# Feed-forward parts of 4, 8, 6 and 4 hidden tiles in a four-layer decoder trunk

## The chip, the cores and the metric

The kernel runs on one core of a Trainium2 chip. The metric is the device time of one execution in microseconds (us); lower is better. Engines: PE is TensorE (matmuls), DVE is VectorE, ACT is ScalarE, POOL is GpSimd, SP is SyncE, which here only issues transfers.

## The reference, cut to what matters

```python
for i in range(4):                       # D = 1024, 512 tokens, one sequence
    h = rmsnorm(x, mix_norm[i])
    x = x + mixer_i(h)                   # i = 0, 3: sparse attention; 1: gated MLP; 2: causal pooling
    x = x + swiglu(rmsnorm(x, ffn_norm[i]), w_gate_up[i], w_down[i])
return rmsnorm(x, final_norm)

def swiglu(h, w_gate_up, w_down):        # 2816 hidden = 22 tiles of 128
    g, u = jnp.split(h @ w_gate_up, 2, axis=-1)
    return (silu(g) * u) @ w_down
```

All of it is float32.

## The kernel before

**Numbers.** A float32 operand is cut into a high part (an ACT copy, rounded) and a low part (a DVE subtraction), and every product is three matmuls: high by high, high by low, low by high (`mm3`, line 2058). Activations stand transposed: a tile is 128 features by 512 tokens. Weights come from memory as 128 rows of up to 1024 columns: DMA into `raw`, ACT writes `w_hi` (line 731), DVE writes `w_lo` (line 1215). There are four such weight slots and four PSUM banks for their results (`RING`), and two slots of `raw`.

**The feed-forward of a layer** goes over its 22 hidden tiles in four parts, `PARTS`. Part 0 (4 tiles) is plain: 8 up blocks of 8 tiles each, then 8 down blocks of 4 tiles each, every matmul 512 columns wide (`first_tiles`, `first_down`). The ups of parts 1, 2 and 3, and the downs of parts 1 and 2, are done with seven products in place of eight (a Strassen-Winograd scheme over 2 by 2 blocks): 256 tokens per matmul, products named s1, s2, a11, s4, s3, a12, a22 (`pair`, line 2172). One up pair is 7 x 4 x 3 = 84 matmuls and makes one hidden tile; one down pair makes two output tiles and is 7 x (half the part's tiles) x 3 matmuls, 63 with a part of 6. The first down pair of a part runs its products in the order s1, a11, s2, s4, s3, a12, a22 (`FIRST_DOWN`), because s2 needs sums of the hidden tile finished last. Those sums and their splits are made by DVE and ACT: `joined` (lines 1461, 1466), `token_sums` (1475 to 1482), `operand_high` (864 to 872), `token_low` (1490), `low` (1503). The weights of a pair are summed and split in four chunks: `pair_sums` (1307, 1309), `pair_high` (787), `pair_low` (1315); GpSimd issues DMAs that add in memory (683, 685).

**The down of part 3** is plain again, eight blocks of (part 3's tiles) x 3 matmuls of 512 columns, with `project`. In this stretch DVE goes, for output tile k, through: the residual (line 1619, one operand in PSUM), the weight split of block k + 3 (line 1215), and the low part of the next norm's input (`xs_low`, line 1223). For k = 3 and k = 7 the last two change places:

```python
if last or k % RING < RING - 1:
    ahead_of(k)
if not last:
    dve.wait_ge(taken, b + 1)
    xs_low(n + 1, k, k + MT * (n + 1))
    if k % RING == RING - 1:
        ahead_of(k)
```

ACT makes the high parts between (lines 731 and 740). GpSimd squares each tile as soon as its residual is in and adds it up (`squares`, lines 627 and 629; 636 for the first). PE opens block b only when its weights are split and when the bank's output of block b - 4 has been taken (`open_block`, line 2067). The mixer that follows reads `xs_lo` tile by tile; the sum of squares is used in its second block. In the last layer there is no `xs_low`; DVE squares tile 7 itself, behind a wait for all of GpSimd's squares (lines 2035 and 2036).

**SBUF.** `xs_hi` and `xs_lo` (8 tiles each) hold the token sums of the hidden tiles in their first 6 tiles and, in tile 7, the high part of one block of tokens, `b21_hi`. `vbd_all` holds attention's compressed values; it is zeroed once, at the start.

Of the kernel before, what the change touches and what calls it, by code (L numbers as in the profile page):

```python
# [25 lines left out]
F32R = mybir.dt.float32r  # L26
# [6 lines left out]
P = 128  # L33
S = 512
D = 1024
MT = D // P
TT = S // P
HEADS, GROUPS, DH = 16, 4, 64
NCMP = 32
HIDDEN_TILES = 22  # L40
PARTS = (4, 6, 6, 6)
TILES_AT = (0, 4, 10, 16)
LAST_PART = len(PARTS) - 1
FIRST_TILES = PARTS[0]
SEQ = [(kind, p, j) for p in range(1, LAST_PART + 1) for kind, n in (("up", PARTS[p]), ("down", MT // 2 * (p < LAST_PART)))
# [5 lines left out]
H = 256  # L51
# [218 lines left out]
def build(nc, x_in, positions, stream, pairs, params, consts, b_s, out, mixers=MIXERS):  # L270
    plan = Plan(mixers)
    ctx = ExitStack()
    with ctx:
# [7 lines left out]
        def over(name, shape, base, at, dt=F32):  # L281

            return nc.alloc_sbuf_tensor_at(name, shape, dt, offset=home[base] + 4 * at)

        def sem(name):
# [53 lines left out]
        t32 = over("t32", [P, 4, 4, H], "mix_lo", 0)  # L339
        part_sums, lin = over("part_sums", [P, 4, H], "tmp", 0), over("lin", [P, 3, H], "tmp", 4 * H)  # L340
        acts = [over("act_e", [P, S], "vstat", 0), over("act_o", [P, S], "hid_lo", (MT - 1) * S)]
        ht32 = over("ht32", [P, 3, 4, H], "xs_lo", 0)

        bank = [ctx.enter_context(nc.psum_tensor(f"bank{i}", [P, S], F32)) for i in range(4)]
        pair = ctx.enter_context(nc.psum_tensor("bank45", [P, 2, S], F32))
# [29 lines left out]

        t_hi = mix_hi[:, :, :].rearrange("p (i k) (h t) -> p i (k h) t", i=4, h=2)
        t_lo = mix_lo[:, :, :].rearrange("p (i k) (h t) -> p i (k h) t", i=4, h=2)
        b21_hi = [xs_hi[:, MT - 1, :].rearrange("p (k t) -> p k t", k=2),
                  xs_lo[:, MT - 1, :].rearrange("p (k t) -> p k t", k=2)]

        ht_hi, ht_lo = (t[:, 0:6, :].rearrange("p (i k) (h t) -> p i (k h) t", i=3, h=2) for t in (xs_hi, xs_lo))

        def hid_11(t, i):

            return t[:, 3 + i // 2, bass.ts(i % 2, H)]

        def f32(ap):
            return ap.bitcast(F32)
# [233 lines left out]
        def _(gp):  # L622
# [72 lines left out]
                    gp.wait_ge(cs_added, e + 1)  # L695
                    nc.gpsimd.tensor_tensor(osum, osum, branch[:, 2, :], ALU.add).then_inc(osum_ready, 1)

            gp.memset(vbd_all[:, :, :, :].rearrange("p g j v -> p (g j v)"), 0.0).then_inc(vbd_zero, 1)
            gp.wait_ge(vbd_zero, 1)
            for j in range(4):  # L700
                gp.memset(vbd_all[NCMP * j:NCMP * (j + 1), :, j, DH:VW], 1.0).then_inc(vbd_zero, 1)
            gp.wait_ge(vbd_zero, 5)
            a = 0
            for l, (kind, _) in enumerate(plan.mixers):
                if norm_of_mixer(l) in cols_of:
                    columns(norm_of_mixer(l))
                if kind == "nsa":
                    nsa(l, a)
                    attention(l, a)
                    a += 1  # L710
                squares(norm_of_ffn(l))
                weight_sums(l)
                squares(norm_of_ffn(l) + 1)
# [1340 lines left out]
        def _(pe):  # L2054
# [3 lines left out]
            def mm3(out_, w, v, start, stop, onto=False):  # L2058

                mm(out_, w[0], v[0], start, False, onto)  # L2060
                mm(out_, w[0], v[1], False, False, onto)
                return mm(out_, w[1], v[0], False, stop, onto)
# [4 lines left out]
            def open_block(b):  # L2067

                pe.wait_ge(w_lo_ready, b + 1)
                if not (type(b) is int and b < RING):  # L2070
                    pe.wait_ge(taken, b - RING + 1)
# [148 lines left out]
            def ffn(l):  # L2220
                n, up = norm_of_ffn(l), plan.ffn[l]

                def amid(k):
                    if k == 2:
                        norm(n)

                project(up, up % RING, MT, xs, (xs_lo_ready, MT * n))
                for b in range(up + 1, up + 2 * FIRST_TILES):
                    project(b, b % RING, MT, xs, before=amid if b == up + 1 else None)
                first_down(l)  # L2230
                for r in range(LAYER_PAIRS):
                    pair(l, r)
                down, t0 = plan.down_block(l, LAST_PART), HIDDEN_TILES * l + TILES_AT[LAST_PART]
                for b in range(down, down + MT):
                    project(b, b % RING, PARTS[LAST_PART], hid, (hid_lo_ready, t0) if b == down else None)

            def values(b0, banks, amid={}, ready=None, spare=0, done=None):

# [507 lines left out]
```

## Time and profile before

| | |
|---|---|
| median of 3 runs | 2320.01 us (2317.48 to 2321.12) |
| the profiled execution | 2318.43 us, its span 2316.3 us |
| PE busy | 2299.5 us (99%), 15224 matmuls |
| DVE, ACT, POOL busy | 1846.0 (80%), 1249.0 (54%), 485.0 us (21%) |
| granted TensorE clock | 9 tenths or more in every slice (mean share 1.0) |
| DMA | 293.12 MB, mean 127 GB/s |

The busy time of PE sums matmuls whose modelled ends overlap, so 99% does not say that PE is at its peak. What one matmul costs in a stream is the distance between two starts in the timeline, and a wait is a distance that is longer than that. The seven-product stretches start at 414.9, 898.2, 1342.2 and 2026.6 us of the span.

### The profile page before, as it was taken

How to read it: one execution, taken by the hardware profiler on the slowest of the kernel's cores; microseconds unless marked ns; L12 is line 12 of the kernel's file. 1: busy time of each engine (PE TensorE's matmuls, PEld its weight loads, DVE VectorE, ACT ScalarE, POOL GpSimd, SP SyncE). 2: the span in 40 equal slices, each digit the busy share in tenths (PEclk: the TensorE clock that was granted, in tenths of full speed). 3: DMA queues.
4: the chain of work that ended last, by engine and by line, in shares of the span. 5: the costliest groups of instructions: out<-in, count | busy, mean ns of one | idle time of the engine just before them, and what ended most of it. 6: DMA issues, size and time to landing. Idle time of an engine off the chain costs nothing.

```text
span 2316.3 us, 41517 instructions
## 1 busy us (share of the span) xinstructions
PE 2299.5 (99%) x15224; PEld 2106.4 (91%) x15224; DVE 1846.0 (80%) x3231; ACT 1249.0 (54%) x2208; POOL 485.0 (21%) x513
## 2 busy tenths in 40 slices
PE   9999999999999999999999999999999999999998
PEld 7889988999988889999988899999889998899997
DVE  8667668899975678999787889997756776989984
ACT  6268744566543344665533455654426783466653
POOL 2211141121130130111133111113320114012112
PEclk9999999999999999999999999999999999999999
DMA  4810014676733245677433467673470002367672
GB/s 162 228 57 2 1 58 120 169 177 167 199 105 109 91 123 140 165 185 192 119 98 101 123 165 177 167 192 110 127 207 29 2 2 94 108 169 185 167 181 91
DMA packets 114242, 293.12 MB, mean 127 GB/s; under 512 B 13184, under 2 KB 25600, under 8 KB 114048
## 3 DMA queue, kind: packets, MB, share of 16 engines
q1 hardware_dynamic: 77904, 229.57, 30.7%
q0 software_dynamic: 35136, 58.74, 15.4%
q8 instruction: 123, 2.02, 0.4%
q10 hardware_dynamic: 1008, 2.21, 0.3%
q14 instruction: 71, 0.58, 0.1%
HBM read 279.98 MB, written 2.10 MB: 122 GB/s over the span
## 4 chain that ended last, share of the span: by engine, by line
PE 92%; DVE 4%; DMA 2%; issue 1%; ACT 1%; SPq 0%; DVEq 0%; ACTq 0%
PE bank L2056 88%; PE bank L2407 3%; DMA raw_b<-pairs 1%; DVE w_lo L1315 1%; DVE act_o L1466 0%; DMA x<-x_in 0%; DVE lin L1588 0%; ACT w_hi L787 0%; DVE lin L1461 0%; DVE xs_lo L1490 0%; PE bank L2437 0%; DVE ht L1479 0%; DVE ht L1477 0%; DVE lin L1593 0%; DVE branch L1821 0%
## 5 line engine op out<-in xcount | busy, mean ns | idle before, releaser
L2056 PE MATMUL bank<-mix_hi,w_hi 128*128 128x256 f32 (+1 forms) x1408 | 428.0, 304 | 0.3
L2056 PE MATMUL bank<-mix_hi,w_lo 128*128 128x256 f32 (+1 forms) x1408 | 425.7, 302 | 0.0
L2056 PE MATMUL bank<-mix_lo,w_hi 128*128 128x256 f32 (+1 forms) x1408 | 425.7, 302 | 0.0
L2056 PE MATMUL bank<-xs_hi,w_hi 128*128 128x512 f32 (+2 forms) x1184 | 412.1, 348 | 6.1 <-DVE xs_lo L1490 5.2
L2056 PE MATMUL bank<-xs_lo,w_hi 128*128 128x512 f32 (+2 forms) x1184 | 404.5, 342 | 0.0
L2056 PE MATMUL bank<-xs_hi,w_lo 128*128 128x512 f32 (+1 forms) x1168 | 398.5, 341 | 0.0
L731 ACT ACTIVATE w_hi<-raw 128x1024 fp32r<-128x1024 f32 (+2 forms) x196 | 186.0, 950 | 229.8 <-DMA raw<-stream 186.1
L1215 DVE TENSOR_TENSOR w_lo<-raw,w_hi 128x1024 fp32r<-128x1024 f32 (+2 forms) x193 | 229.5, 1191 | 95.9 <-ACT w_hi L731 95.3
L857 ACT ACTIVATE part_sums<-bank 128x256 f32<-128x256 f32 x416 | 155.3, 379 | 269.8 <-PE bank L2056 221.7
L2056 PEld LDWEIGHTS bank<-mix_hi,w_hi 128*128 128x128 f32 x1408 | 269.1, 191 | 12.4 <-DVE w_lo L1315 2.2
L2056 PEld LDWEIGHTS bank<-mix_hi,w_lo 128*128 128x128 f32 x1408 | 269.1, 191 | 10.1
L2056 PEld LDWEIGHTS bank<-mix_lo,w_hi 128*128 128x128 f32 x1408 | 269.2, 191 | 9.8
L2056 PEld LDWEIGHTS bank<-xs_hi,w_hi 128*128 128x128 f32 (+1 forms) x1184 | 224.0, 189 | 37.4 <-DVE xs_lo L1490 8.2
L2056 PEld LDWEIGHTS bank<-xs_lo,w_hi 128*128 128x128 f32 (+1 forms) x1184 | 223.4, 189 | 26.3 <-issue 1.0
L2056 PE MATMUL bank<-b_lo,w_hi 128*128 128x256 f32 x864 | 244.5, 283 | 0.0
L2056 PEld LDWEIGHTS bank<-xs_hi,w_lo 128*128 128x128 f32 x1168 | 221.4, 190 | 25.2
L1315 DVE TENSOR_TENSOR w_lo<-s,w_hi 128x512 fp32r<-128x512 f32 (+1 forms) x208 | 185.7, 893 | 42.7 <-ACT w_hi L787 40.2
L2056 PE MATMUL bank<-hid_hi,w_hi 128*128 128x512 f32 (+1 forms) x624 | 212.2, 340 | 0.0
L2056 PE MATMUL bank<-hid_lo,w_hi 128*128 128x512 f32 (+1 forms) x624 | 212.2, 340 | 0.0
L2056 PE MATMUL bank<-hid_hi,w_lo 128*128 128x512 f32 (+1 forms) x624 | 212.2, 340 | 0.0
L787 ACT ACTIVATE w_hi<-s 128x512 fp32r<-128x512 f32 (+1 forms) x208 | 164.2, 790 | 47.3 <-DVE s L1309 24.8
L1797 DVE CUSTOM_DVE_ANT_0 attn<-bank,causal_b 128x512 f32<-128x512 f32 (+3 forms) x256 | 118.8, 488 | 84.5 <-PE bank L2056 83.8
(279 smaller groups left out, 5114.1 us busy)
## 6 DMA issues: line engine op xcount, KB each, us to landing
raw<-stream SPq DMA_DIRECT2D x131, 512.0 KB, 3.5
raw_b<-pairs SPq DMA_DIRECT2D x72, 512.0 KB, 5.1
raw_a<-pairs SPq DMA_DIRECT2D x72, 512.0 KB, 5.3
s<-pairs SPq DMA_DIRECT2D x72, 256.0 KB, 4.2
s<-pairs POOLq DMA_DIRECT2D x72, 256.0 KB, 7.0
raw_b<-pairs SPq DMA_DIRECT2D x32, 384.0 KB, 4.2
raw_a<-pairs SPq DMA_DIRECT2D x32, 384.0 KB, 4.4
raw<-stream SPq DMA_DIRECT2D x32, 384.0 KB, 3.1
```

Of the source, the lines that this page charges most:

```text
L731: nc.scalar.activation(w_hi[:, slot, 0:n], raw[:, k, 0:n], ACT.Copy).then_inc(w_hi_ready, 1)
L787: nc.scalar.activation(chunk(l, r, c)[0], chunk_from(r, c), ACT.Copy).then_inc(sw_hi_ready, 1)
L857: nc.scalar.activation(part_sums[:, i, :], src[:, 0:H], ACT.Copy).then_inc(snapped, 1)
L1215: nc.vector.tensor_tensor(w_lo[:, slot, 0:n], raw[:, k, 0:n], f32(w_hi[:, slot, 0:n]), ALU.subtract).then_inc(w_lo_ready, counted(b))
L1315: nc.vector.tensor_tensor(lo, chunk_from(r, c), f32(hi), ALU.subtract).then_inc(sw_lo_ready, 1)
L1797: nc.vector.tensor_tensor_reduce(out=prob[:, p % 4, bass.ts(j, w)], in0=bank[score_bank(l0, p)][:, bass.ts(j, w)], in1=causal_b[:, S - w:S ...
L2056: return nc.tensor.matmul(out_, w, v, start=start, stop=stop, skip_group_check=onto)
L2407: last = nc.tensor.transpose(bank[turn_bank(l0, p)][:, bass.ts(k, P)], prob[:, p % 4, bass.ts(k, P)], ident[:, :])
```

## The change

Part 1 gets 8 tiles in place of 6, and part 3 gets 4 in place of 6. With 8 tiles the token sums take all of `xs_hi` and `xs_lo`, so `b21_hi` moves into `vbd_all`; GpSimd therefore zeroes that buffer again ahead of the second attention layer. The first two blocks of the last down are interleaved: three tiles of the one, three of the other, then the fourth tile of each.

```diff
-PARTS = (4, 6, 6, 6)
-TILES_AT = (0, 4, 10, 16)
+PARTS = (4, 8, 6, 4)
+TILES_AT = (0, 4, 12, 18)
...
-        ht32 = over("ht32", [P, 3, 4, H], "xs_lo", 0)
+        ht32 = over("ht32", [P, 4, 4, H], "xs_lo", 0)
...
-        b21_hi = [xs_hi[:, MT - 1, :].rearrange("p (k t) -> p k t", k=2),
-                  xs_lo[:, MT - 1, :].rearrange("p (k t) -> p k t", k=2)]
-
-        ht_hi, ht_lo = (t[:, 0:6, :].rearrange("p (i k) (h t) -> p i (k h) t", i=3, h=2) for t in (xs_hi, xs_lo))
+        b21_all = over("b21_all", [P, 4, H], "vbd_all", 0, F32R)
+        b21_hi = [b21_all[:, 2 * k:2 * k + 2, :] for k in range(2)]
+
+        ht_hi, ht_lo = (t[:, :, :].rearrange("p (i k) (h t) -> p i (k h) t", i=4, h=2) for t in (xs_hi, xs_lo))
...
-            return t[:, 3 + i // 2, bass.ts(i % 2, H)]
+            return t[:, 4 + i // 2, bass.ts(i % 2, H)]
...
+            def empty_vbd(l, a):
+
+                if l:
+                    gp.wait_ge(product_done, 7 * LAYER_PAIRS * l)
+                gp.memset(vbd_all[:, :, :, :].rearrange("p g j v -> p (g j v)"), 0.0).then_inc(vbd_zero, 1)
+                gp.wait_ge(vbd_zero, 5 * a + 1)
+                for j in range(4):
+                    gp.memset(vbd_all[NCMP * j:NCMP * (j + 1), :, j, DH:VW], 1.0).then_inc(vbd_zero, 1)
+                gp.wait_ge(vbd_zero, 5 * (a + 1))
...
+                    empty_vbd(l, a)
                     nsa(l, a)
...
-                for b in range(down, down + MT):
-                    project(b, b % RING, PARTS[LAST_PART], hid, (hid_lo_ready, t0) if b == down else None)
+                last, early = PARTS[LAST_PART] - 1, range(down, down + (3 if PARTS[LAST_PART] == 2 else 2))
+                for b in early:
+                    open_block(b)
+                    for k in range(last):
+                        pe.wait_ge(hid_lo_ready, t0 + k + 1)
+                        mm3(bank[b % RING][:, :], wslot(b % RING, k * P), hid(k), k == 0, False)
+                pe.wait_ge(hid_lo_ready, t0 + PARTS[LAST_PART])
+                for b in early:
+                    mm3(bank[b % RING][:, :], wslot(b % RING, last * P), hid(last), False, True).then_inc(block_done, 1)
+                for b in range(down + len(early), down + MT):
+                    project(b, b % RING, PARTS[LAST_PART], hid)
```

PE at the start of layer 0's last down, before; `bank2` is its first block, `bank3` its second, and three matmuls make one hidden tile:

```order
L2056 MATMUL bank2<-hid_hi,w_hi 128x512 [waits hid_lo_ready,taken,w_lo_ready]
L2056 MATMUL bank2<-hid_lo,w_hi 128x512
L2056 MATMUL bank2<-hid_hi,w_lo 128x512
L2056 MATMUL bank2<-hid_hi,w_hi 128x512 [waits hid_lo_ready]
...
L2056 MATMUL bank3<-hid_hi,w_hi 128x512 [waits taken,w_lo_ready]
...
L2056 MATMUL bank0<-hid_hi,w_hi 128x512 [waits taken,w_lo_ready]
```

The same place in the changed kernel, where lines stand 6 further down:

```order
L2062 MATMUL bank2<-hid_hi,w_hi 128x512 [waits hid_lo_ready,taken,w_lo_ready]
...
L2062 MATMUL bank3<-hid_hi,w_hi 128x512 [waits hid_lo_ready,taken,w_lo_ready]
...
L2062 MATMUL bank2<-hid_hi,w_hi 128x512 [waits hid_lo_ready]
L2062 MATMUL bank2<-hid_lo,w_hi 128x512
L2062 MATMUL bank2<-hid_hi,w_lo 128x512
L2062 MATMUL bank3<-hid_hi,w_hi 128x512
...
L2062 MATMUL bank0<-hid_hi,w_hi 128x512 [waits taken,w_lo_ready]
```

The second block is opened 9 matmuls behind the first instead of 18, and the fourth tile of both comes after six tiles of work.

DVE in the same down, output tiles 2 to 4, before:

```order
L1619 TENSOR_TENSOR x<-x,bank 128x512 [waits block_done,taken]
L1215 TENSOR_TENSOR w_lo<-raw,w_hi 128x768 [waits w_hi_ready]
L1223 SCALAR_TENSOR_TENSOR xs_lo<-x,par,xs_hi 128x512 [waits xs_hi_ready,taken]
L1619 TENSOR_TENSOR x<-x,bank 128x512 [waits block_done,taken]
L1223 SCALAR_TENSOR_TENSOR xs_lo<-x,par,xs_hi 128x512 [waits xs_hi_ready,taken]
L1215 TENSOR_TENSOR w_lo<-raw,w_hi 128x768 [waits w_hi_ready]
L1619 TENSOR_TENSOR x<-x,bank 128x512 [waits block_done,taken]
```

And in the changed kernel:

```order
L1625 TENSOR_TENSOR x<-x,bank 128x512 [waits block_done,taken]
L1221 TENSOR_TENSOR w_lo<-raw,w_hi 128x512 [waits w_hi_ready]
L1229 SCALAR_TENSOR_TENSOR xs_lo<-x,par,xs_hi 128x512 [waits xs_hi_ready,taken]
L1625 TENSOR_TENSOR x<-x,bank 128x512 [waits block_done,taken]
L1229 SCALAR_TENSOR_TENSOR xs_lo<-x,par,xs_hi 128x512 [waits xs_hi_ready,taken]
L1221 TENSOR_TENSOR w_lo<-raw,w_hi 128x512 [waits w_hi_ready]
L1625 TENSOR_TENSOR x<-x,bank 128x512 [waits block_done,taken]
```

The order on DVE is as it was; only the splits of the last down's weights are narrower.

## Rows read from the trace of the kernel before

**Rows 1.** Waits of PE: engine, line, waited for: us in total, times, longest

```profile
PE bank L2056 <- DVE xs_lo L1490: 5.2, 8, 0.7
```

**Rows 2.** Timeline of PE, layer 0: start us, us, engine, line, operation

```profile
565.79 0.28 PE L2056 MATMUL bank<-xs_lo,w_lo 128*128 128x256 f32 x1
565.91 0.28 PE L2056 MATMUL bank<-xs_lo,w_hi 128*128 128x256 f32 x1
...
659.58 0.40 PE L2056 MATMUL bank<-hid_hi,w_hi 128*128 128x512 f32 x1
...
692.25 0.39 PE L2056 MATMUL bank<-w_hi,xs_hi 128*128 128x512 f32 x1
```

**Rows 3.** Timeline of PE, first down pair of part 2, layer 0

```profile
570.47 0.28 PE L2056 MATMUL bank<-xs_hi,w_lo 128*128 128x256 f32 x1
571.40 0.39 PE L2056 MATMUL bank<-xs_hi,w_hi 128*128 128x256 f32 x1 [0.65 <-DVE xs_lo L1490]
571.62 0.28 PE L2056 MATMUL bank<-xs_lo,w_hi 128*128 128x256 f32 x1
```

**Rows 4.** Timeline of DVE, same place, two weight splits ahead of it

```profile
563.53 0.55 DVE L1315 TENSOR_TENSOR w_lo<-s,w_hi 128x384 fp32r<-128x384 f32 x1
...
566.18 0.96 DVE L1315 TENSOR_TENSOR w_lo<-s,w_hi 128x768 fp32r<-128x768 f32 x1
```

**Rows 5.** Timeline of PE: fifth up pair, layer 0; first up pair behind a down, layer 2

```profile
552.96 0.28 PE L2056 MATMUL bank<-b_hi,w_lo 128*128 128x256 f32 x1
553.22 0.39 PE L2056 MATMUL bank<-mix_hi,w_hi 128*128 128x256 f32 x1
...
1438.51 0.28 PE L2056 MATMUL bank<-b_hi,w_lo 128*128 128x256 f32 x1
1439.41 0.35 PE L2056 MATMUL bank<-b_hi,w_hi 128*128 128x256 f32 x1 [0.63 <-ACT part_sums L857]
```

**Rows 6.** Timeline of DVE, last down of layer 0, output tiles 3 and 5

```profile
676.20 0.69 DVE L1619 TENSOR_TENSOR x<-x,bank 128x512 f32<-128x512 f32 x1 [1.07 <-PE bank L2056]
677.75 1.01 DVE L1223 SCALAR_TENSOR_TENSOR xs_lo<-x,par,xs_hi 128x512 fp32r<-128x512 f32 x1 [0.86 <-ACT xs_hi L740]
678.67 2.04 DVE L1215 TENSOR_TENSOR w_lo<-raw,w_hi 128x768 fp32r<-128x768 f32 x1
680.64 0.68 DVE L1619 TENSOR_TENSOR x<-x,bank 128x512 f32<-128x512 f32 x1
...
684.36 0.69 DVE L1619 TENSOR_TENSOR x<-x,bank 128x512 f32<-128x512 f32 x1 [0.73 <-PE bank L2056]
```

**Rows 7.** Timeline of POOL, same down, and last a row of layer 1's

```profile
677.16 1.04 POOL L627 TENSOR_TENSOR work<-x 128x512 f32 x1 [0.89 <-DVE x L1619]
678.28 1.62 POOL L629 TENSOR_TENSOR work<-work 128x512 f32<-128x512 f32 x1
...
683.16 1.62 POOL L629 TENSOR_TENSOR work<-work 128x512 f32<-128x512 f32 x1
...
1173.40 1.76 POOL L627 TENSOR_TENSOR work<-x 128x512 f32 x1 [0.25 <-POOL work L629]
```

**Rows 8.** Timeline of DVE, layer 1's output projection, residuals of tiles 0 and 1

```profile
799.24 0.69 DVE L1282 TENSOR_TENSOR x<-bank,x 128x512 f32 x1 [4.95 <-PE bank L2056]
...
802.43 0.68 DVE L1282 TENSOR_TENSOR x<-bank,x 128x512 f32 x1
```

**Rows 9.** Groups of DVE by form: xcount | busy us, mean ns | idle before, releaser

```profile
L1315 DVE TENSOR_TENSOR w_lo<-s,w_hi 128x512 fp32r<-128x512 f32 x72 | 49.3, 685 | 0.2
```

**Rows 10.** Timelines of POOL and DVE at the end of the last down of layer 3

```profile
2302.25 1.29 POOL L629 TENSOR_TENSOR work<-work 128x512 f32<-128x512 f32 x1
...
2304.98 0.69 DVE L2036 TENSOR_TENSOR work<-x 128x512 f32<-128x512 f32 x1
```

**Rows 11.** DMA issues: engine, operation xcount, KB each, median us to landing

```profile
raw<-stream SPq DMA_DIRECT2D x34, 256.0 KB, 2.8
```

**Rows 12.** Groups of POOL, columns as in rows 9

```profile
L698 POOL MEMSET vbd_all<- 128x1040 f32 x1 | 1.0, 965 | 0.3 <-POOLq L2738 0.3
```

More of the change, by code:

```diff
@@ L696, in attention @@
                     nc.gpsimd.tensor_tensor(osum, osum, branch[:, 2, :], ALU.add).then_inc(osum_ready, 1)
[L698 to L702, printed above, removed]
+            def empty_vbd(l, a):
[6 more added lines that the diff above has]
+                gp.wait_ge(vbd_zero, 5 * (a + 1))
             a = 0
```

## The prediction
> **What bounds the kernel now.** PE does. The waits of PE come first: they sum to about 10 us in the whole span, over half of it one wait, eight times, at the first down pair of parts 1 and 2 [rows 1]. The timeline of PE then gives the price of a matmul as the distance of two starts: 0.120 us with 256 columns (565.79 to 565.91), and with 512 columns 32.67 us for the 144 of a last down (659.58 to 692.25), 0.227 us each [rows 2]. The last down shows no wait at all. So the change is priced by PE's matmuls, by PE's few waits, and by the question whether DVE, ACT, GpSimd and the transfers keep up once the last down goes by in two thirds of the time. For that I read DVE's and POOL's timelines side by side.
>
> **Matmuls.** Per layer the last down loses 2 tiles x 8 blocks x 3 = 48 matmuls of 512 columns, 48 x 0.227 = 10.9 us. The downs of part 1 gain 4 pairs x 7 x 1 x 3 = 84 of 256 columns, 84 x 0.120 = 10.1 us. Ups: 18 tiles before and after. Saved: 0.8 us a layer, **-3.2 us** in all. A rule speaks against the trade: the Trainium skill, page "TensorE: Matmul & The Clock Gate", section "Back-to-back issue gap", gives about 81 ns sustained for 128 columns and 131 ns for 512; with these the 48 would be worth 6.3 us and the 84 cost at least 6.8, a loss of 0.5 us or more a layer. The trace has 227 ns for 512, and the measurement decides.
>
> **First down pair of part 1.** Now s2's last hidden tile is reached after 8 x 3 = 24 matmuls, 2.88 us into the pair, and starts 0.93 us behind its neighbour where 0.12 is due [rows 3]: 0.81 us, 0.10 more for the refill (the next start comes 0.22 later), and 0.25 of the same kind further on, 1.15 in all; each of the 8 such pairs has it. With 8 tiles it is reached after 33 matmuls, 3.96 us. But DVE's way there gets longer [rows 4]: three operations of 384 columns become 512 (0.55 to 0.69) and two splits of 768 become 1024 (0.96 to 1.23), together +0.96, and DVE works there without a pause. The part now comes 3.69 us into the pair, then 4.65. Left: 0.69 + 0.10. Saved 0.35 a layer, **-1.4 us**.
>
> **Ups.** DVE lags in a run of ups; the fifth pair of part 1 or 2 pays 0.26 - 0.12 + 0.10 = 0.24 us [rows 5]. With eight pairs the seventh pays too: **+1.0 us**. Behind the short down pairs (63 matmuls, 7.56 us) the first up pair waits for sums in two of the layers, at most 0.90 - 0.12 = 0.78 us [rows 5], because its full-width transfers have less time than between ups. Down pairs of part 1 now last 10.08 us, as ups do; this and what follows in that run (0.7 and 1.2 us in layers 1 and 2) should go: **-1.9 us**. Nothing of it goes behind part 2.
>
> **The last down, where I expect the time to go.** DVE and POOL hardly overlap there. POOL's square of 1.04 us ends at 678.20 and DVE's xs_lo, under way since 677.75, ends 0.56 later; the addition runs 678.28 to 679.90, and the split begun at 678.67 takes 2.04 instead of 0.96, ending 0.81 behind it [rows 6, 7]. The other way round the addition takes 1.62 where it takes 1.29 alone [rows 7, 10]. The residual, with an operand in PSUM, is not slowed: 0.69 at 684.36 inside an addition. So split and xs_lo queue with POOL's 1.04 + 1.29 us per tile. The Trainium skill, "GPSIMD Engine Reference", section "8. Key points", says the same: GpSimd shares its SBUF interfaces with VectorE, and instructions with two SBUF inputs contend. The trace agrees, as above.
>
> A block of 4 tiles is 12 x 0.227 = 2.72 us. One turn of DVE is a residual (0.69), a split (0.69 at 512 columns [rows 9]), and an xs_lo no sooner than 1.55 us behind the residual (676.20 to 677.75, ACT's high part between). In the output projection, with all inputs waiting, a turn takes 802.43 - 799.24 = 3.19 us with a split of 1024 [rows 8]. And turn 3, where xs_lo stands ahead of the split, takes 680.64 - 676.20 = 4.44 with no pause at its end [rows 6]. Before, PE gave each turn 4.08 us, and three blocks of lead took the 4.44.
>
> Walked through with these durations and no overlap, from the start of the down: blocks 0 and 1 end at 4.76 and 5.44, residuals start at 5.0, 7.8, 10.5, 13.6 and 18.2. Turn 3, as an example: POOL adds from 13.5 to 14.8 and squares tile 3 from 15.0 to 16.1; xs_lo, due at 15.2, ends at 16.6; POOL's next addition runs 16.5 to 17.8; the split, due at 16.6, ends at 18.3 (less than 0.69 is left of it behind POOL, as in rows 6). The split of block 6 comes behind turn 3's xs_lo, at 18.3; PE wants it at 6 x 2.72 = 16.3. **Stall 2.0.** Residuals 5, 6, 7 then start at 21.0, 26.2, 29.4 (the splits are 1024 wide again), the next mixer's first weights are ready at 24.5 against 23.8 (0.7), and its first block wants input tiles 6 and 7 before they are there (0.9 and 2.3, tile 7 at 32.5). That is 5.9 us where a projection follows (pooling, second attention). The gated MLP's first block wants the banks, not the late tiles: 2.0 + 0.7 + 1.6 = 4.3. Three layers: **+16.1 us**. Bounds from the nearest rows: with each turn no slower than in this trace (2.3, 2.9, 2.9, 4.2), block 6 stalls 0.9 and the sum is 2.6, 2.6 and 1.4 us, **+6.6**; with 3.2 for every turn and the rest as walked, about 8, 8 and 6, **+22**. I take the walk: the same walk with 6 tiles and 4.08 us a block puts residuals 3, 4 and 5 at 16.6, 21.0 and 24.8, where the trace has 16.6, 21.1 and 24.8 (676.20, 680.64 and 684.36 less 659.58), is 0.65 late in turn 6, and has no stall.
>
> In the last layer there is no xs_lo, but POOL needs 1.04 + 1.29 and gaps of 0.08 and 0.25 [rows 7], 2.66 a tile, plus the splits it waits for, and a block gives 2.72. Its last addition, now 0.2 us ahead of the end of the down (2303.54 [rows 10]), ends about 1.9 behind it in the walk. DVE's square of tile 7 waits for it: it starts 2.0 instead of 1.0 behind the end. **+1.0 us.**
>
> **At nothing.** Zeroing `vbd_all` again is 0.97 us and four small ones on POOL [rows 12], behind the squares of layer 2; POOL has nothing to do there until attention's first rows are in. The wait it adds is for products long done. Block 1's weights are wanted at 2.04 instead of 4.08: DVE's split ends at about 1.95, so cover is thin; if gone, 0.1 to 0.3 us a layer. The fourth hidden tile is wanted at 4.08, ready at 2.7. Transfers: the last down asks for 256 KB per 2.72 us where it asked for 384 KB per 4.08, the same rate, and 256 KB land in 2.8 us [rows 11], inside the two blocks between reuse of a slot.
>
> **Sum.** 2318.4 - 3.2 - 1.4 + 1.0 - 1.9 + 16.1 + 1.0 = 2330.0 for an execution like the profiled one, which is 1.6 us under the median. Against the median of 2320.0: **2331 us**, +11, 0.5% slower.
>
> **Rivals.** (1) DVE's lag is milder, as in the lower bound: -5.5 + 6.6 + 1.0 = +2.1, 2322 us. For it: in this trace POOL pauses between tiles and often meets no split. Against: with 2.7 us a block it has no pauses. A chance of 0.17. (2) The other side: the three blocks of lead absorb the lag. If block 6's split comes by 16.3 us and tile 7 before the next block wants it, only the first four terms are left: 2320.0 - 5.5 = 2314.5 us. For it: without POOL a turn is 2.3 us, under 2.72. Against: the 4.44 us turn is already over PE's pace of 4.08. 0.15. (3) The change doesn't do what it says: the up pair behind part 1 waits as before, since its transfers and not the pair's length bind it, and the eighth up leaves DVE further behind. That is +2 to +4 us on any case; with the forecast 2334. 0.13, slower. (4) The last down as walked or worse: 0.55, up to 2337.
>
> **Numbers.** A measurement of this kernel tells 0.2% (4.6 us) from no change, so same is 2315.4 to 2324.6. Slower: 0.68 (the forecast and rival 3). Same: 0.17. Faster: 0.15. The range leaves out most of rival 2 and the outer end of the bounds: 2318 to 2338.
>
> **What would show it.** Starts of PE inside each seven-product pair still 0.120 apart, and 12 matmuls to a product in part 1's downs instead of 9. In the three inner last downs a gap of about 2 us ahead of the seventh block, waited for on DVE's w_lo; residuals of tiles 3 and 4 about 4.6 us apart and the others 2.7 to 3.2; a wait on xs_lo of line 1229 in the first block of pooling and of the second attention, 2 to 3 us. In the last layer no gap in the down and the square of tile 7 one us later. Wrong it is if the last downs run through in 21.8 us with no wait behind them, or if the up run of part 1 shows waits much over 0.25 us.

## The result and the profile after

| | before | changed |
|---|---|---|
| median | 2320.53 us, 6 runs (2317.48 to 2321.19) | 2333.66 us, 6 runs (2332.52 to 2337.63) |
| profiled execution (its span) | 2318.43 us (2316.3) | 2332.81 us (2330.7) |
| PE, matmuls | 2299.5 us busy, 15224 | 2299.5 us busy, 15368 |
| DVE, ACT, POOL busy | 1846.0, 1249.0, 485.0 us | 1871.5, 1259.5, 483.4 us |

The change makes the kernel slower by 0.6%: the ratio is 1.0061, 95% interval 1.0048 to 1.0074. From the starts of PE, the four layers' seven-product stretches, last downs, and what follows up to the next such stretch (or the end) took, in us:

| | layer 0 | layer 1 | layer 2 | layer 3 | sum of differences |
|---|---|---|---|---|---|
| seven products | 244.67, now 255.30 | 245.35, 254.42 | 246.90, 254.57 | 244.72, 254.71 | +37.4 |
| last down | 32.67, now 24.40 | 32.67, 24.40 | 32.67, 24.40 | 32.68, 23.79 | -33.7 |
| behind it | 205.98, now 207.47 | 165.97, 170.45 | 404.81, 409.45 | 12.28, 12.35 | +10.7 |

The matmuls alone are +40.3 (336 x 0.120) and -43.5 (192 x 0.227). So the last downs hold 9.8 us that no matmul explains, and what follows them 10.7.

PE's waits in the changed kernel: engine, line, waited for: us in total, times, longest. The row of rows 1 is the third here.

```profile
PE bank L2062 <- DVE w_lo L1221: 6.7, 7, 1.7
PE bank L2062 <- DVE xs_lo L1229: 6.4, 6, 2.0
PE bank L2062 <- DVE xs_lo L1496: 3.6, 8, 0.7
PE bank L2062 <- POOL work L629: 1.8, 1, 1.8
```

Weights and inputs split by DVE have become the largest waits, and one is for GpSimd itself. Where they stand, in PE's timeline (start us, us, engine, line, operation, idle before and releaser), first around layer 0's last down, then layer 1's:

```profile
670.26 0.40 PE L2062 MATMUL bank<-hid_hi,w_hi 128*128 128x512 f32 x1
...
688.56 0.50 PE L2062 MATMUL bank<-hid_hi,w_hi 128*128 128x512 f32 x1 [1.73 <-DVE w_lo L1221]
694.67 0.50 PE L2062 MATMUL bank<-w_hi,xs_hi 128*128 128x512 f32 x1 [0.33 <-DVE w_lo L1221]
700.14 0.50 PE L2062 MATMUL bank<-w_hi,xs_hi 128*128 128x512 f32 x1 [1.10 <-DVE x L1625]
...
1174.86 0.50 PE L2062 MATMUL bank<-hid_hi,w_hi 128*128 128x512 f32 x1 [1.73 <-DVE w_lo L1221]
1180.96 0.50 PE L2062 MATMUL bank<-xs_hi,w_hi 128*128 128x512 f32 x1 [0.36 <-DVE w_lo L1221]
1185.83 0.50 PE L2062 MATMUL bank<-xs_hi,w_hi 128*128 128x512 f32 x1 [0.49 <-DVE xs_lo L1229]
1188.74 0.80 PE L2062 MATMUL bank<-xs_hi,w_hi 128*128 128x512 f32 x1 [1.95 <-DVE xs_lo L1229]
```

The first wait stands ahead of the seventh block, the second at the next mixer's first weights, the others in its first block. Layer 2 repeats layer 1 (2.12, 0.73, 0.87 and 2.33 us as distances of two starts). The same down on DVE, output tiles 3 and 4, and the row that ends the wait (with rows 6, 9):

```profile
683.84 0.67 DVE L1625 TENSOR_TENSOR x<-x,bank 128x512 f32<-128x512 f32 x1
685.38 1.46 DVE L1229 SCALAR_TENSOR_TENSOR xs_lo<-x,par,xs_hi 128x512 fp32r<-128x512 f32 x1 [0.86 <-ACT xs_hi L746]
686.76 1.74 DVE L1221 TENSOR_TENSOR w_lo<-raw,w_hi 128x512 fp32r<-128x512 f32 x1
688.43 0.67 DVE L1625 TENSOR_TENSOR x<-x,bank 128x512 f32<-128x512 f32 x1
```

And on POOL:

```profile
685.25 1.04 POOL L627 TENSOR_TENSOR work<-x 128x512 f32 x1 [0.18 <-POOL work L629]
686.37 1.59 POOL L629 TENSOR_TENSOR work<-work 128x512 f32<-128x512 f32 x1
```

The split of block 6's weights, 0.69 us alone [rows 9], takes 1.74 beside POOL's addition and ends at 688.50; PE goes on at 688.56. In this turn POOL passes from one tile to the next with 0.18 us between, where it idled 0.89 [rows 7]; ahead of tiles 1, 4 and 6 it still idles 1.4 us, waiting for DVE's residual.

### The profile page after: what moved, and what is told of

It reads as the page before. It is cut to its first block, busy times and chain, and to the rows that moved or that the text cites. A ratio compares the mean times of both kernels' runs of the same rounds, so it can differ in the third digit from the quotient of the medians.

```text
span 2330.7 us, 41863 instructions
## 1 busy us (share of the span) xinstructions
PE 2299.5 (99%) x15368; PEld 2107.7 (90%) x15368; DVE 1871.5 (80%) x3259; ACT 1259.5 (54%) x2220; POOL 483.4 (21%) x518
## 4 chain that ended last, share of the span: by engine, by line
PE 83%; DVE 8%; issue 4%; DMA 2%; ACT 2%; POOL 1%; DVEq 0%; SPq 0%; POOLq 0%; ACTq 0%
PE bank L2062 79%; PE bank L2422 3%; DVE w_lo L1321 1%; DMA raw_b<-pairs 1%; DVE xs_lo L1229 1%; ACT w_hi L793 1%; DVE act_o L1472 1%; DVE lin L1594 1%; DVE w_lo L1221 1%; DVE x L1625 0%; DMA raw<-stream 0%; DVE lin L1467 0%; DMA x<-x_in 0%; ACT xs_hi L746 0%; DVE ht L1485 0%
## 5 line engine op out<-in xcount | busy, mean ns | idle before, releaser
L2062 PE MATMUL bank<-xs_hi,w_hi 128*128 128x512 f32 (+1 forms) x1104 | 390.9, 354 | 11.3 <-DVE xs_lo L1229 6.4
L2062 PE MATMUL bank<-xs_lo,w_hi 128*128 128x512 f32 (+1 forms) x1104 | 383.1, 347 | 0.0
L2062 PE MATMUL bank<-xs_hi,w_lo 128*128 128x512 f32 (+1 forms) x1088 | 376.9, 346 | 0.0
L737 ACT ACTIVATE w_hi<-raw 128x1024 fp32r<-128x1024 f32 (+1 forms) x196 | 179.1, 915 | 217.2 <-DMA raw<-stream 172.1
L1221 DVE TENSOR_TENSOR w_lo<-raw,w_hi 128x1024 fp32r<-128x1024 f32 (+1 forms) x193 | 224.2, 1164 | 90.0 <-ACT w_hi L737 89.4
L2062 PEld LDWEIGHTS bank<-xs_hi,w_hi 128*128 128x128 f32 x1104 | 209.2, 190 | 44.6 <-DVE xs_lo L1229 7.8
L2062 PEld LDWEIGHTS bank<-xs_lo,w_hi 128*128 128x128 f32 x1104 | 208.8, 189 | 26.2 <-issue 1.0
L2062 PE MATMUL bank<-hid_hi,w_hi 128*128 128x256 f32 (+1 forms) x608 | 201.9, 332 | 6.0 <-DVE w_lo L1221 5.2
L2062 PE MATMUL bank<-hid_lo,w_hi 128*128 128x256 f32 (+1 forms) x608 | 201.0, 331 | 0.0
L2062 PE MATMUL bank<-hid_hi,w_lo 128*128 128x256 f32 (+1 forms) x608 | 200.9, 330 | 0.0
```

Of the source, the lines that this page charges most:

```text
L737: nc.scalar.activation(w_hi[:, slot, 0:n], raw[:, k, 0:n], ACT.Copy).then_inc(w_hi_ready, 1)
L1221: nc.vector.tensor_tensor(w_lo[:, slot, 0:n], raw[:, k, 0:n], f32(w_hi[:, slot, 0:n]), ALU.subtract).then_inc(w_lo_ready, counted(b))
L2062: return nc.tensor.matmul(out_, w, v, start=start, stop=stop, skip_group_check=onto)
```

## Experiments

Each kernel is the changed one with the edit shown, unless it says otherwise. The changed kernel's 2333.66 us is what medians are compared with; ratios are to the kernel before, run beside each of them. Its median was 2320.5 us in the runs of the result and 2319.5 to 2320.1 in those of the experiments, so a difference of one microsecond between medians of different runs says nothing by itself; for small ones the starts in the traces are read.

**GpSimd's squares shortened.** Is it GpSimd at all?

```diff
-                gp.tensor_tensor(work2[:, 0, :], tile(x, m), tile(x, m), ALU.mult).then_inc(sq_step, 1)
+                gp.tensor_tensor(work2[:, 0, 0:c], x[:, m, 0:c], x[:, m, 0:c], ALU.mult).then_inc(sq_step, 1)
...
-                gp.tensor_tensor(work[:, 0, :], work[:, 0, :], work2[:, 0, :], ALU.add).then_inc(sq_step, 1)
+                gp.tensor_tensor(work[:, 0, 0:c], work[:, 0, 0:c], work2[:, 0, 0:c], ALU.add).then_inc(sq_step, 1)
...
-                squares(norm_of_ffn(l) + 1)
+                squares(norm_of_ffn(l) + 1, 8)
```

> Leaves out part of the computation: in the last down of each layer GpSimd squares and adds 8 of 512 columns of tiles 1 to 7 (tile 0 in full), so the next norm's sum of squares is left out for the other columns. Theory A (GpSimd's squares and DVE's low parts and splits exclude each other in SBUF, and that makes the lag): a DVE turn falls to 0.69 + 0.69 + 0.74 = 2.1 us, under the 2.72 us of a block; the waits of 2.1 and 0.7 us (three layers), 0.9 + 2.3 us (two layers), 1.4 us (the first) and the 1.8 us for POOL in the last layer go: 18.1 us, and 2.5 us of half-clock matmuls behind the longest waits with them. Total 15 to 21 us less than the changed kernel, 2316. Rival B (DVE's or ACT's own work does not fit into a block of 12 matmuls, GpSimd is no matter): the waits stay, and the total falls by under 4 us.

Measured: 2313.81 us, 11 runs, ratio 0.9977 (0.9968 to 0.9986). This kernel leaves out part of the sums of squares, so it is a measurement and no replacement. The last downs take 21.85 us each, with no wait left inside but one of 0.05; behind them 0.7 us of waits on xs_lo remain. The same place on DVE:

```profile
681.44 0.68 DVE L1625 TENSOR_TENSOR x<-x,bank 128x512 f32<-128x512 f32 x1
682.98 0.75 DVE L1229 SCALAR_TENSOR_TENSOR xs_lo<-x,par,xs_hi 128x512 fp32r<-128x512 f32 x1 [0.86 <-ACT xs_hi L746]
683.65 0.69 DVE L1221 TENSOR_TENSOR w_lo<-raw,w_hi 128x512 fp32r<-128x512 f32 x1
684.25 0.68 DVE L1625 TENSOR_TENSOR x<-x,bank 128x512 f32<-128x512 f32 x1
```

The same order of work, 2.81 us from residual to residual instead of 4.59: xs_lo 0.75 for 1.46, the split 0.69 for 1.74, the residual as it was. That is the contention, measured by taking it away; with GpSimd's own lateness at the end of layer 3 it is 19.9 us of the run.

**ACT squares, GpSimd only adds.**

```diff
+                if not by_act:
+                    wait_x(gp, n, m)
...
-                squares(norm_of_ffn(l) + 1)
+                squares(norm_of_ffn(l) + 1, True)
...
+                    if 0 < k < (MT if n + 1 < plan.norms - 1 else MT - 1):
+                        wait_x(act, n + 1, k)
+                        act.wait_ge(sq_step, 2 * k + FIRST_SQUARES + SQUARES * n - 1)
+                        nc.scalar.activation(work2[:, 0, :], x[:, k, :], ACT.Square).then_inc(sq_step, 1)
```

> The changed kernel, complete, but ACT squares tiles 1 to 7 in the last down and GpSimd only adds them up (1.3 to 1.6 us per tile instead of 2.6 to 3.2). Theory A (what counts is how long GpSimd holds SBUF against DVE): half of its time there goes, ACT gets 0.6 us per tile to its 1.35, still under 2.72; two thirds of the waits go, 9 to 15 us, total 2321. Rival B (ACT becomes late with the high parts of weights and tiles, since its square stands ahead of the next block's high part): waits on w_lo and xs_lo stay as long, total within 3 us of 2333.7.

Measured: 2321.88 us, ratio 1.0014 (1.0005 to 1.0023); 11.8 us less, as theory A said. Last downs 22.2 to 22.5 us. What is left: 0.5 and 0.6 us in the gated MLP's first blocks, and 0.3, 0.4 and 1.4 us in each of the two other mixers, on w_lo and then on xs_lo of tiles 6 and 7. In the last layer PE now waits 0.2 us for POOL instead of 1.8, but the end comes 14.0 us behind the down instead of 12.4.

**DVE splits first.**

```diff
-                    if last or k % RING < RING - 1:
-                        ahead_of(k)
+                    ahead_of(k)
                     if not last:
                         dve.wait_ge(taken, b + 1)
                         xs_low(n + 1, k, k + MT * (n + 1))
-                        if k % RING == RING - 1:
-                            ahead_of(k)
```

> The changed kernel, but DVE splits block k + 3's weights ahead of the low part of the next norm's input for every k, also for k = 3 and 7. Theory A (DVE's order decides which wait comes): the seventh block's weights are ready one low part sooner (1.2 to 1.5 us), so the 2.1 us ahead of it fall to about 0.7; the 0.7 us ahead of the next mixer's first block go; the low part of tile 7 comes 0.7 us later in layers 1 and 2. Total 3 to 6 us less than the changed kernel, 2329. Rival B (the seventh block waits for ACT's high part of the weights, which comes behind the end of block 2, or for the transfer): nothing moves, within 0.5 us of 2333.7.

Measured: 2330.85 us, ratio 1.0052 (1.0038 to 1.0065); 2.8 less, just short of the 3 to 6 expected. The wait ahead of the seventh block is gone altogether, but it comes back behind the down: the last row here was 1.95 us.

```profile
1176.11 0.50 PE L2059 MATMUL bank<-xs_hi,w_hi 128*128 128x512 f32 x1 [0.23 <-DVE w_lo L1221]
1181.24 0.50 PE L2059 MATMUL bank<-xs_hi,w_hi 128*128 128x512 f32 x1 [0.76 <-DVE xs_lo L1229]
1184.92 0.50 PE L2059 MATMUL bank<-xs_hi,w_hi 128*128 128x512 f32 x1 [2.71 <-DVE xs_lo L1229]
```

The order decides where the lag is paid, and little of how much there is. In the middle of the down DVE then runs at its own pace, residuals 3.15 us apart where PE needs 2.72:

```profile
1167.45 0.68 DVE L1625 TENSOR_TENSOR x<-x,bank 128x512 f32<-128x512 f32 x1
1168.05 1.18 DVE L1221 TENSOR_TENSOR w_lo<-raw,w_hi 128x512 fp32r<-128x512 f32 x1
1169.15 1.52 DVE L1229 SCALAR_TENSOR_TENSOR xs_lo<-x,par,xs_hi 128x512 fp32r<-128x512 f32 x1
1170.60 0.68 DVE L1625 TENSOR_TENSOR x<-x,bank 128x512 f32<-128x512 f32 x1
```

**Without the interleaving.** The last down's blocks in plain order, as before the change.

```diff
-                last, early = PARTS[LAST_PART] - 1, range(down, down + (3 if PARTS[LAST_PART] == 2 else 2))
...
+                for b in range(down, down + MT):
+                    project(b, b % RING, PARTS[LAST_PART], hid, (hid_lo_ready, t0) if b == down else None)
```

> The changed kernel with the last down's blocks in their plain order (no interleaving). In the changed kernel's trace the low part of the fourth hidden tile ends 2.81 us behind the start of layer 0's last down (673.07 against 670.26); in the plain order PE wants it after nine matmuls, 2.04 us, so a wait of 0.75 us per layer appears in the first block, 3.0 us in all (less the 0.05 us that the second block's weights cost now). In return block 0 ends at 3.5 us instead of 4.8, and its residual, split and GpSimd's first square start 1.3 us sooner. Theory A (the loss is DVE, ACT and GpSimd lagging behind a shorter down): the 2.1 us ahead of the seventh block shrinks by 1.3 to 2.0 us in the three inner layers, the next mixer's waits stay within 0.5 us; total 2.0 us less than the changed kernel, 2331.7, bounds -5 to +1. Rival B (the interleaving is needed and the lag is set by PE's own pace): the 2.1 us stay and the total is 2.8 us more, 2336.5.

Measured: 2331.35 us, 2.3 less. The wait for the fourth hidden tile is there (1.03 us between two starts, 0.8 more than due), and the first residual starts 3.9 us behind the down's start (673.30 less 669.36) instead of 5.1. The wait ahead of the seventh block falls from 1.9 to 0.15 us in layers 0 and 2, to 1.15 in layer 1, where a split and an xs_lo of the second turn run beside POOL and take 1.54 and 1.77 us. The interleaving hides one wait and makes a longer one: it delays the first output, on which DVE, ACT and GpSimd start. By the ratios alone (1.0053, 1.0039 to 1.0067, against 1.0061) the two kernels can't be told apart; the starts of PE show both effects, and in the two traces the last downs are 1.5 us shorter together and what follows them 0.6.

**One tile lent.** Block 1 gives block 0 one hidden tile of cover instead of three.

```diff
+                open_block(down + 1)
+                part_of(down + 1, (0,))
+                pe.wait_ge(hid_lo_ready, t0 + last + 1)
+                part_of(down, (last,)).then_inc(block_done, 1)
+                part_of(down + 1, range(1, last + 1)).then_inc(block_done, 1)
```

> The changed kernel with one edit: the second block of the last down lends the first only one hidden tile (three matmuls) instead of three tiles. The plain order cost 0.8 us of wait for the fourth hidden tile per layer and won 2.3 us in all, since the first residual came 1.3 us sooner. Theory A (DVE and GpSimd start the last down's work too late; each 1 us of earlier start is 1 us of less wait further on): both advantages, the first residual 0.7 us later than in the plain order, no wait of 0.8 us; 1 to 3 us below the plain order's 2331.4, so 2329.4. Rival B (the first residual's time is no matter, the plain order was better by chance of the DMA): 2333.

Measured: 2331.03 us, ratio 1.0052 (1.0038 to 1.0067) against the plain order's 1.0053. Miss: the wait of 0.8 us is down to 0.1, but 0.8, 1.8 and 0.8 us stand ahead of the seventh blocks, where the plain order had 0.15, 1.15 and 0.15. The cover took nothing from the lead: in layer 0 the first residual starts 3.94 us behind the down's start in both kernels, the later residuals at the same distances to 0.03 us too, and the seventh block 17.4 us behind it, here (down's start 669.28) and there (669.36):

```profile
686.71 0.50 PE L2062 MATMUL bank<-hid_hi,w_hi 128*128 128x512 f32 x1 [0.69 <-DVE w_lo L1221]
```

```profile
686.78 0.50 PE L2062 MATMUL bank<-hid_hi,w_hi 128*128 128x512 f32 x1
```

DVE's turns set that time, and they start with the first residual. So what PE saves in the first block it waits for again ahead of the seventh, and the cover is worth nothing there; only the last layer's down gets shorter by it, 23.48 us for 23.91.

**The next mixer's first two blocks together.** Tiles 0 to 5 of both, then 6 and 7 of both.

```diff
+                for part in (range(0, MT - 2), range(MT - 2, MT)):
+                    for z in range(2):
+                        if not part[0]:
+                            open_block(b0 + z)
+                        for k in part:
...
+                            end = mm3(bank[(b0 + z) % RING][:, :], wslot((b0 + z) % RING, k * P), xs(k), k == 0,
+                                      k == MT - 1)
```

> The changed kernel; in the mixer that follows a last down PE takes tiles 0 to 5 of its first two blocks first and tiles 6 and 7 of both after them (in the gated MLP the fourth quarter of the tokens, whose bank is free last, comes behind three quarters of the next block). Lagging DVE is left as it is, only the inputs that come late are wanted later. Theory A (PE idles for xs_lo tiles 6 and 7, nothing else is late there): the waits of 0.9 and 2.3 us in layers 2 and 3's mixers and 1.3 us in layer 1's go, with the 1 to 1.6 us at half clock behind them; 7.5 to 9.5 us less than the changed kernel, 2325. Rival B (the sum of squares or the row of scales, wanted in the second block, is then what is late, since GpSimd is behind as well): half of it comes back as a wait for POOL or DVE, 2329.

Measured: 2332.87 us, ratio 1.0056 (1.0042 to 1.0069); 0.8 less, no difference that medians can show. Theory A falls, and nearly all comes back, more than the half of rival B: the waits on xs_lo are down from 6.4 to 0.4 us, and the sum of squares, 10 tiles into the mixer, is not there.

```profile
1180.63 0.50 PE L2062 MATMUL bank<-xs_hi,w_hi 128*128 128x512 f32 x1 [0.35 <-DVE w_lo L1221]
1189.55 1.05 PE L2062 MATMUL bank<-ones,work 128*128 128x2 f32 x8 [1.81 <-POOL work L629]
```

POOL was as late as DVE; the wait on xs_lo had hidden it.

**Parts of 4, 8, 4, 6.** Keeps the large part and the moved block, and gives the last down its 6 tiles back.

```diff
-PARTS = (4, 8, 6, 4)
-TILES_AT = (0, 4, 12, 18)
+PARTS = (4, 8, 4, 6)
+TILES_AT = (0, 4, 12, 16)
```

> The changed kernel with parts of 4, 8, 4 and 6 tiles: part 1 as large as in the change, the last down as long as before (6 tiles), and as many matmuls as before. Theory A (the loss sits in the last down of 4 tiles alone): no wait on w_lo or xs_lo in the last downs, none for POOL at the end; the up pairs take 10.04 us instead of 10.08 as in the changed kernel (72 of them, 2.9 us), the down pairs of part 2 have 42 matmuls (5.04 us) and their sums and splits 1 to 2 us per layer more of waits. Total within -3 to +3 us of before, best guess 2318. Rival B (the part of 8 tiles or the moved token block costs by itself): over 2325.

Measured: 2338.30 us, ratio 1.0079 (1.0066 to 1.0093), a miss of 20, but not where rival B has it. The last downs take 32.67 us again, and what follows 205.95, 165.96 and 406.17. That is no loss but for 1.4 us in the second attention, where PE once waits 1.2 us for ACT far behind the last down. Part 1's ups and downs are as in the change. The four down pairs of part 2, 42 matmuls or 5.04 us each, take 7.6, 5.7, 6.1 and 7.1 to 7.4, 6.5 us more a layer than their matmuls, where I allowed 1 to 2. A down pair has work on DVE that does not shrink with the part, and DVE goes with hardly a pause, 6.13 us from pair to pair, of which it is busy 5.96:

```profile
588.14 0.42 DVE L1547 TENSOR_TENSOR x<-x,lin 128x256 f32<-128x256 f32 x1
...
594.27 0.42 DVE L1547 TENSOR_TENSOR x<-x,lin 128x256 f32<-128x256 f32 x1
```

So the shorter last down is the place of the change's loss, and a down pair of 4 tiles is no way round it.

**The kernel before with the token block moved.**

```diff
-        b21_hi = [xs_hi[:, MT - 1, :].rearrange("p (k t) -> p k t", k=2),
-                  xs_lo[:, MT - 1, :].rearrange("p (k t) -> p k t", k=2)]
+        b21_all = over("b21_all", [P, 4, H], "vbd_all", 0, F32R)
+        b21_hi = [b21_all[:, 2 * k:2 * k + 2, :] for k in range(2)]
...
+                    empty_vbd(l, a)
```

> The kernel before with one thing of the change: b21_hi in vbd_all, and the zeroing of vbd_all ahead of the second attention. In the changed kernel's trace the product a12, which reads b21_hi, takes 1.416 us instead of 1.440, the product behind it 1.424. Theory A (the place of the operand in SBUF makes its matmuls 2 to 3 ns shorter): the 72 up pairs take 10.04 us instead of 10.08, 2.9 us less than before, 2316.6. Rival B (the shorter pairs come from something else, parts or timing): the pairs stay at 10.08 and the total within 0.5 us of before.

Measured: 2317.62 us, ratio 0.9993 (0.9984 to 1.0002): unclear. The up pairs are 10.04 us apart (434.76 to 444.80) where they were 10.08 (435.07 to 445.15), so theory A holds for the matmuls: the product a12 takes 1.416 us, the one behind it 1.424. But the first down pairs take 8.79 us instead of 8.71, the fifth up pairs of part 1 10.40 instead of 10.30 to 10.33, and the four seven-product stretches of that execution 983.3 us where they were 981.6. So PE's gain of 2.9 us is not seen in the stretch; that DVE, with less time per pair, takes it back fits these pairs but was not tested, and this execution, at 2319.66, is one of the slower ones of its kernel.

**All repairs.** ACT's squares, splits first, one tile lent, the mixers' blocks together.

> All repairs together: ACT squares, DVE splits first for every k, the next mixer's first two blocks together, and the second block of the last down lends the first only one hidden tile (three matmuls, 0.68 us: with the nine ahead 2.7 us of cover against 2.8), so that the first residual comes 1.4 us sooner. Theory A (every stall comes from the same lag and the cures add up): of the 9.0 us of waits that the kernel with ACT's squares still shows in and behind the last downs 5 to 7 go, total 2316, bounds 2313 to 2319, at or below before. Rival B (with the squares on ACT, ACT is the late engine): 2321 as with ACT's squares alone.

Measured: 2317.01 us, ratio 0.9989 (0.9980 to 0.9998), as theory A had it. Last downs 22.0 us, then 205.96, 167.33 and 404.75. Longer than before are the end, 14.1 us behind the last down, and what follows layer 1's, by 1.4 us: PE waits 1.3 us in pooling for mix_lo.

**And the final scale in step.** In the last layer ACT makes each scaled copy right behind its residual.

```diff
+                    else:
+                        wait_x(act, n + 1, k)
...
+                        nc.scalar.activation(xg[:, k, :], x[:, k, :], ACT.Copy, scale=g_of(n + 1, k)
+                                             ).then_inc(xg_ready, 1)
```

> All repairs, and in the last layer ACT's eight scaled copies for the output (xg) each behind its residual instead of all behind the squares. In the trace with all repairs these eight run 5.0 us in a row from 2299.53 to 2304.55, and the square root's table load comes after them; before the change it came 0.75 us behind the last residual. The end behind the last down falls from 14.1 us to 12.3: 1.7 us less, 2315.3, bounds 2313.5 to 2317. Rival: PE's sum of squares, which waits for GpSimd's last addition, sets the end, and under 0.7 us is won.

Measured: 2315.75 us, ratio 0.9984 (0.9975 to 0.9994), as expected, though the intervals of the two kernels overlap. The end comes 12.31 us behind the down, 1.7 sooner, but the down of layer 3 ends 0.6 us later (22.96 for 22.37, with the wait behind it): PE waits 0.8 us for POOL's last addition where it waited 0.2.

**The same, mixers as in the changed kernel.** The blocks together are taken out again.

> All repairs and the final scale, without taking the next mixer's first two blocks together. Theory A (with the squares on ACT and the first residual sooner DVE ends each last down hardly behind PE): tile 7's low part is still wanted 4.8 us behind the down's end, waits of 0.5 to 1 us each in layers 1, 2 and 3's mixers come back; 1 to 3 us above the kernel with everything, 2317.3. Rival B (it was the interleaving of the mixers that cured it): 4.7 us or more above.

Measured: **2314.69 us** (2313.59 to 2315.78), ratio 0.9979 (0.9969 to 0.9988): the lowest of the complete kernels, and faster than both, by 0.2% than the kernel before. Theory A is not borne out: it is 1.1 us below the kernel with the blocks together, not above, though the intervals overlap. Of PE's waits these three belong to the last downs and what stands behind them:

```profile
PE bank L2065 <- POOL work L630: 0.8, 1, 0.8
PE bank L2065 <- DVE xs_lo L1235: 0.7, 3, 0.3
PE bank L2065 <- DVE w_lo L1227: 0.5, 1, 0.5
```

Once nothing lags, the blocks together cure nothing, and in the trace with them PE waits 1.3 us in pooling for mix_lo, which it doesn't here. The same place on DVE as above, 2.67 us from residual to residual (4.59 in the changed kernel):

```profile
680.96 0.68 DVE L1631 TENSOR_TENSOR x<-x,bank 128x512 f32<-128x512 f32 x1
681.56 1.18 DVE L1227 TENSOR_TENSOR w_lo<-raw,w_hi 128x512 fp32r<-128x512 f32 x1
682.67 0.74 DVE L1235 SCALAR_TENSOR_TENSOR xs_lo<-x,par,xs_hi 128x512 fp32r<-128x512 f32 x1
683.63 0.69 DVE L1631 TENSOR_TENSOR x<-x,bank 128x512 f32<-128x512 f32 x1 [0.22 <-PE bank L2065]
```

It waits for PE again, 0.22 us, instead of PE for it.

**All repairs with parts of 4, 6, 6, 6.**

> All repairs and b21_hi in vbd_all, but parts of 4, 6, 6 and 6 tiles. Theory A (the parts of 4, 8, 6, 4 are worth their arithmetic once nothing lags: 0.8 us per layer of matmuls and 0.3 to 0.4 us of the first down pair, 4.6 us in all; the repairs give nothing where no engine lags): near the 2317.6 of the kernel before with b21_hi moved, within 1.5 us, and 2 to 5 us above the same repairs with parts of 4, 8, 6, 4. Rival B (the gain comes from the repairs, whatever the parts): at or below it.

Measured: 2320.42 us, ratio 1.0000 (0.9991 to 1.0009), 4.7 above the same kernel with parts of 4, 8, 6, 4. With the old parts the repairs give nothing, so rival B falls; with the new ones the kernel is faster, by the medians as much as the arithmetic of the parts promises (4.6). The two profiled executions are only 2.4 us apart (spans 2317.3 and 2314.9), 2.2 of it in the seven products and last downs, so the size is less sure than the sign. The distance to 2317.6 was foreseen as at most 1.5 and is 2.8; the intervals of the two ratios overlap (1.0000, 0.9991 to 1.0009, and 0.9993, 0.9984 to 1.0002), so it is no difference that these runs can show.

## Why the prediction was right

Forecast 2331, measured 2333.66; the change in the profiled execution was forecast as +11.6 and was +14.4 us. Term by term:

| term | forecast | measured |
|---|---|---|
| matmuls | -3.2 | -3.2 |
| first down pair of part 1 | -1.4 | -1.1 (0.87 us a pair in excess, was 1.15) |
| seventh up pair | +1.0 | +1.3 |
| up pairs behind part 1's down | -1.9 | -1.8 |
| last downs and the blocks behind them | +16.1 | +15.0 of waits, +3.4 more, most of it at half clock |
| tail | +1.0 | +2.0 |
| not foreseen in the seven products | 0 | -2.3 (up pairs 0.04 shorter), +1.0 (other pairs) |
| sum | +11.6 | +14.4 |

The mechanism is the one forecast, in the places forecast. That the total came out 2.8 us off and not more is in part luck: the 3.4 us at half clock and the 1.0 in the tail, which the sum did not hold, are met by 1.1 us less of waits and by the shorter pairs.

**The last down** went as walked. Residuals 0 to 4 start 5.1, 7.8, 10.4, 13.6 and 18.2 us behind its start (675.38 to 688.43 less 670.26), forecast 5.0, 7.8, 10.5, 13.6 and 18.2; the last ones 20.8, 26.0 and 29.2 (21.0, 26.2, 29.4). The stall ahead of block 6 is 2.12 - 0.23 + 0.11 = 2.0 us in each of the three (the distance of two starts, less the one that is due, and 0.11 by which the next start comes late as well); at the next mixer 0.6 (0.7), then 0.75 and 2.1 (0.9 and 2.3) in pooling and the second attention, 1.4 (1.6) in the gated MLP. That the two engines' times add up is shown by these starts; that this is what the change loses by was tested three ways: GpSimd's work taken away (-19.9 us), halved (-11.8), and left with DVE's order changed (-2.8).

**Rivals.** The milder lag (1) and the absorbing lead (2) are excluded by the waits above. The reason given against rival 1, that POOL would have no pauses, is itself only half true: it idles 1.4 us ahead of three tiles, and the walk held all the same. Rival 2's 2314.5 is close to the 2314.7 of the complete kernel that repairs the lag, but not by its arithmetic alone: the shorter up pairs are in that time and were not in the sum. Its condition was false. Rival 3 fails: behind part 1's downs the first up pairs take 10.04 us in all layers.

**The tail was mis-sized.** I let DVE's square of tile 7 wait for POOL and priced that. It does, 1.0 us later. But PE waits for the same addition ahead of its sum of the first seven tiles, and the transposes and the sum of the eighth stand in its queue behind that. The place in the changed kernel:

```profile
2316.16 0.39 PE L2062 MATMUL bank<-hid_hi,w_lo 128*128 128x512 f32 x1
2318.33 1.05 PE L2062 MATMUL bank<-ones,work 128*128 128x2 f32 x8 [1.78 <-POOL work L629]
2319.24 1.07 PE L2605 MATMUL bank<-ident,xg 128*128 128x128 f32 x8
2320.15 0.95 PE L2062 MATMUL bank<-ones,work 128*128 128x2 f32 x8
```

POOL ended 1.9 us behind the down, as walked; the step missed is who waits for it: two engines, and PE's queue is the longer way.

**At nothing.** Block 1's weights cost 0.05 us a layer, the fourth hidden tile and the transfers nothing on PE. But I gave the interleaving no price against the plain order: it moves the first residual 1.2 us back, worth some 2 us (2.3 by the medians, which can't tell it from nothing; 2.1 by the last downs and what follows them in the two traces).

## What to carry to other kernels

When a stage is made shorter on its bound engine, add up per turn what the other engines do in it, with their times beside each other and not alone; where GpSimd works beside DVE instructions with two SBUF operands, add their times. A cure that moves the consumer of late data later uncovers the next late thing, while one that takes work off the late engines cures all waits behind them at once. An order that hides a wait at the head of a stage can delay the first output on which everybody else starts; and where the others' turns set the time, a wait hidden at the head comes back further on.

## What was not expected of the hardware

**The clock falls behind waits.** After the waits of pooling's first block, PE's granted clock is 0.50 for two microseconds, the lower level of 1.2 GHz (stretch: us, busy us of PE, PEld, DVE, ACT, POOL, then PEclk, DMA share, GB/s):

```profile
1174.90:1180.20 5.30, 5.30 (x23) 4.38 (x24) 3.71 (x5) 2.46 (x4) 4.18 (x4) 1.00 0.63 198
1186.40:1189.30 2.90, 0.95 (x3) 0.50 (x2) 2.07 (x2) 2.26 (x3) 2.64 (x3) 0.84 0.21 85
1189.30:1191.40 2.10, 2.10 (x6) 1.65 (x5) 2.10 (x5) 0.80 (x1) 0.52 (x1) 0.50 0.00 0
1191.40:1195.00 3.60, 3.60 (x20) 3.10 (x19) 2.42 (x8) 0.21 (x1) 0.00 (x0) 0.94 0.81 251
```

There matmuls of 512 columns start 0.43 us apart:

```profile
1189.76 0.63 PE L2062 MATMUL bank<-xs_hi,w_lo 128*128 128x512 f32 x1
1190.19 0.63 PE L2062 MATMUL bank<-xs_hi,w_hi 128*128 128x512 f32 x1
```

The Trainium skill, "TensorE: Matmul & The Clock Gate", section "Wait — 56ns, not 53.3ns?", gives 426.7 ns for 512 columns at the low level, and the trace agrees; for the high level it gives 215.7, where this kernel has 227. Eight such matmuls behind layer 2's waits cost 8 x 0.20 = 1.6 us, some 3 us in the two layers, which no term of mine held. It is not the same every time. With the last down in plain order and the same two waits (0.87 and 2.35 us in both mixers), the first stretch here, behind layer 1's, has full clock, the second, behind layer 2's, half:

```profile
1187.30:1192.00 4.70, 4.70 (x25) 3.98 (x26) 4.25 (x11) 1.55 (x3) 1.03 (x1) 1.00 0.33 96
1636.50:1640.00 3.50, 3.50 (x11) 2.71 (x10) 2.91 (x4) 0.95 (x1) 1.89 (x6) 0.51 0.23 44
```

What decides between the two is open. In the kernel before and in those with the squares on ACT or shortened, where no wait here is over 1.4 us, it does not occur at these places.

**An operand's place in SBUF is worth 2% of its matmuls.** With b21_hi in `vbd_all` the 12 matmuls of a12 take 1.416 us instead of 1.440, and the 12 behind them 1.424, in every kernel that has it there and in every layer. Why was not tried.
